# Output sums of a one-core hybrid mixer layer: residual put into the output first, sums added by accumulating transfers, three column blocks emptied by ACT

## What is computed

```
h = rms_norm(x, norm_g[l])
proj = jnp.einsum('bsd,dn->bsn', h, w_in[l])
...
y = jnp.concatenate([y_a, y_b, y_c], axis=-1)
x = x + jnp.einsum('bsm,md->bsd', y, w_out[l])
```

## Time and profile before

| | us |
|---|---|
| median of 3 runs (lowest, highest) | 1533.09 (1531.96, 1533.46) |
| the profiled execution's own time | 1533.12 |
| its span | 1531.3 |
| PE busy | 1524.5 |
| DVE busy | 1050.1 |
| ACT busy | 772.1 |
| POOL busy | 357.1 |

### The profile page before, as it was taken

One profiled execution on the slowest core, in us unless ns is written; L12 is line 12 of the kernel. 1 busy time (PEld: TensorE's weight loads), 2 busy tenths in 40 slices (PEclk: granted clock), 3 DMA queues, 4 the chain that ended last, 5 costly groups with the idle time before them and its releaser, 6 DMA issues.

```text
span 1531.3 us, 18915 instructions
## 1 busy us (share of the span) xinstructions
PE 1524.5 (100%) x6963; PEld 1260.9 (82%) x6963; DVE 1050.1 (69%) x1619; ACT 772.1 (50%) x1025; POOL 357.1 (23%) x605
## 2 busy tenths in 40 slices
PE   9999999999999999999999999999999999999999
PEld 7888888888888887888878888888888888878887
DVE  7647555566769855576579667676556888887884
ACT  6745444587544444554545545534345444454542
POOL 9041112230230040126420354345300011110000
PEclk9999999999999999999999999999999999999999
DMA  9886778886787675569755787798885666677665
GB/s 296 282 244 191 221 212 232 213 234 190 228 248 210 193 223 167 156 183 279 247 187 177 224 253 212 233 274 254 239 261 177 206 197 203 186 263 225 213 224 165
DMA packets 206268, 337.78 MB, mean 221 GB/s; under 512 B 53049, under 2 KB 60520, under 8 KB 205920
## 3 DMA queue, kind: packets, MB, share of 16 engines
q1 hardware_dynamic: 184784, 288.66, 62.2%
q0 software_dynamic: 21344, 47.90, 11.0%
q10 hardware_dynamic: 48, 0.02, 0.0%
HBM read 312.81 MB, written 23.49 MB: 220 GB/s over the span
## 4 chain that ended last, share of the span: by engine, by line
PE 94%; DVE 3%; ACT 1%; DMA 1%; issue 0%; ACTq 0%; DVEq 0%
PE acc L1167 28%; PE acc L1170 28%; PE acc L1169 28%; PE mix L1170 1%; PE mix L1167 1%; PE mix L1169 1%; DVE w_lo L1849 1%; PE mix L1274 1%; PE mix L1357 1%; DVE t_lo L1868 1%; DMA w_raw<-in_w_out_dram 1%; PE mix L1346 0%; PE mix L1267 0%; ACT w_hi L1498 0%; PE acc L1183 0%
## 5 line engine op out<-in xcount | busy, mean ns | idle before, releaser
L1849 DVE TENSOR_TENSOR w_lo<-w_raw,w_hi 128x1024 fp32r<-128x1024 f32 (+2 forms) x524 | 630.3, 1217 | 358.5 <-ACT w_hi L1498 354.7
L1498 ACT ACTIVATE w_hi<-w_raw 128x1024 fp32r<-128x1024 f32 (+2 forms) x524 | 544.0, 1049 | 454.2 <-PE acc L1170 363.6
L1167 PE MATMUL acc<-w_hi,op_hi 128*128 128x512 f32 (+1 forms) x1868 | 734.3, 393 | 0.3 <-DVE w_lo L1849 0.3
L1170 PE MATMUL acc<-w_hi,op_lo 128*128 128x512 f32 (+1 forms) x1868 | 726.9, 389 | 0.0
L1169 PE MATMUL acc<-w_lo,op_hi 128*128 128x512 f32 (+1 forms) x1868 | 726.7, 389 | 0.0
L1167 PEld LDWEIGHTS acc<-w_hi,op_hi 128*128 128x128 f32 x1868 | 350.8, 188 | 74.0 <-issue 1.3
L1170 PEld LDWEIGHTS acc<-w_hi,op_lo 128*128 128x128 f32 x1868 | 350.7, 188 | 73.5
L1169 PEld LDWEIGHTS acc<-w_lo,op_hi 128*128 128x128 f32 x1868 | 350.9, 188 | 71.0
L883 POOL DMA_DIRECT2D conv_dram<-y x48 | 30.7, 692 | 169.3 <-ACT y L1550 168.5
L883 POOL DMA_DIRECT2D y_dram<-y x32 | 20.5, 713 | 185.2 <-DVE y L2362 116.7
L1037 POOL DMA_DIRECT2D bp_dram<-b_ps x48 | 31.1, 694 | 68.6 <-ACT b_ps L1719 64.6
(11 more groups left out here) (467 smaller groups left out, 1295.2 us busy)
## 6 DMA issues: line engine op xcount, KB each, us to landing
w_raw<-in_w_in_dram SPq DMA_DIRECT2D x367, 512.0 KB, 4.6
w_raw<-in_w_out_dram SPq DMA_DIRECT2D x128, 512.0 KB, 4.4
w_raw<-in_w_in_dram SPq DMA_DIRECT2D x16, 384.0 KB, 3.2
w_raw<-in_a_wuq_dram SPq DMA_DIRECT2D x12, 512.0 KB, 5.1
conv_dram<-y POOLq DMA_DIRECT2D x48, 64.0 KB, 3.9
y<-conv_dram POOLq DMA_DIRECT2D x48, 64.0 KB, 4.7
w_raw<-in_a_wuqi_dram SPq DMA_DIRECT2D x6, 512.0 KB, 4.2
bp_dram<-b_ps POOLq DMA_DIRECT2D x48, 64.0 KB, 3.5
```

Source lines behind the costliest of these rows:

```text
L1167: nc.tensor.matmul(o, hi[:, kt, tok], hv[:, i, n0:n1], start=(kt == (kts if late else blk["kts"])[0]), stop=False)
L1170: last_mm = nc.tensor.matmul(o, lo[:, kt, tok], hv[:, i, n0:n1], start=False, stop=(kt == blk["kts"][-1]))
L1498: func(split_ap(w_hi, c), w_raw[:, c % RAW_BUFS, 0:n], ACT.Copy).then_inc(hi_ready, 1)
L1849: vec.tensor_tensor(split_ap(w_lo, c), w_raw[:, c % RAW_BUFS, 0:n], split_ap(w_hi, c).bitcast(F32), ALU.subtract).then_inc(lo_ready, 1)
```

## The change

POOL no longer loads x for seven of the eight column blocks. It copies those seven blocks of x straight into the output in DRAM, in two transfers (256 rows of 6144 bytes and 256 rows of 8192 bytes), where it used to load blocks 0 and 1, and afterwards adds every sum to the output in DRAM by accumulating transfers. Block 3 keeps its load, its adds on DVE and its stores by SP. The results of `out1` and `out2` for blocks 0 to 2 are copied from PSUM by ACT into two staging buffers (`out_stage`), each of which is free again once its accumulating transfer has landed; DVE had added them. `evs` no longer adds x: four DVE adds in place of eight. The two parts of blocks 0 to 2 are transferred one by one, so there are ten accumulating transfers of 512 KB where there were seven stores. The seven-product groups are the same, and so are PE's and SP's instructions.

```diff
-            for n in range(OUT_SINGLE):
-                if 512 * n == W_A:
-                    pool.wait_ge(y_lo_ready, KT // 2 - 4)
-                pool.dma_start(out_acc(n), x_dram[:, :, 512 * n:512 * n + 512]).then_inc(x_again[n], 16)
-            for n in range(2):
-                pool.wait_ge(a_y, 4 * n + 4)
-                y_blocks(n)
-            for p in range(2):
-                if p == 1:
-                    pool.wait_ge(y_lo_ready, KT // 2)
-                for q in range(2):
-                    n = OUT_SINGLE + 2 * p + q
-                    pool.dma_start(pair_sum(p)[:, :, 512 * q:512 * q + 512], x_dram[:, :, 512 * n:512 * n + 512]
-                                   ).then_inc(x_again[n], 16)
+            last_n = OUT_SINGLE - 1
+            for a, z in ((0, 512 * last_n), (512 * last_n + 512, D)):
+                pool.dma_start(out[0][:, a:z], x[0][:, a:z]).then_inc(out_done, 16)
+            pool.wait_ge(y_lo_ready, KT // 2 - 4)
+            pool.dma_start(out_acc(last_n), x_dram[:, :, 512 * last_n:512 * last_n + 512]).then_inc(x_again[last_n], 16)
+            pool.wait_ge(out_done, 32)
+
+            def add_out(k):
+
+                kind, n = ("out1", k) if k < last_n else ("out2", k - last_n)
+                wait_stored(pool, kind, n)
+                if k >= last_n:
+                    pool.wait_ge(out_added[(k - last_n) % 2], 16 * ((k - last_n) // 2 + 1))
+                pool.dma_start(out_dram[:, :, 512 * n:512 * n + 512], out_stage[k % 2], accum_op=ALU.add
+                               ).then_inc(out_added[k % 2], 16)
+
+            add_out(0)
+            add_out(1)
+            pool.wait_ge(a_y, 4)
+            y_blocks(0)
+            add_out(2)
+            pool.wait_ge(a_y, 8)
+            y_blocks(1)
...
-            for n in range(OUT_SINGLE - 1):
-                wait_stored(pool, "out2", n)
-                pool.dma_start(out_dram[:, :, 512 * n:512 * n + 512], out_acc(n)).then_inc(out_done, 16)
-            pool.wait_ge(out_done, 16 * (D // 512 - 1))
+            for k in range(last_n, 2 * last_n):
+                add_out(k)
+            for k in range(2):
+                pool.wait_ge(out_added[k], 16 * last_n)
+            pool.wait_ge(out_done, 16 * (2 + 4))
...
                 if kind in ("out1", "out2"):
+                    if arg == OUT_SINGLE - 1:
+                        return
+                    k = arg if kind == "out1" else OUT_SINGLE - 1 + arg
+                    if k >= 2:
+                        act.wait_ge(out_added[k % 2], 16 * (k // 2))
+                    act.wait_ge(acc_ready, b + 1)
+                    for m in range(M):
+                        ins = func(out_stage[k % 2][:, m, :], acc[b % 2][m][:], ACT.Copy)
...
                 wait_used(dve, last_seven(p))
-                for q in range(2):
-                    dve.wait_ge(x_again[n + q], again_count(n + q))
                 dve.wait_ge(first_kept, p + 1)
-                vec.tensor_tensor(c11, c11, u2, ALU.add)
-                step(vec.tensor_tensor(u2, p6, u2, ALU.add))
+                free(vec.tensor_tensor(u2, p6, u1, ALU.add), 2)
                 free(vec.tensor_tensor(u4, p5, u2, ALU.add), 0)
-                step(vec.tensor_tensor(u3, p7, u2, ALU.add))
-                step(vec.tensor_tensor(u2, p5, u3, ALU.add))
-                free(vec.tensor_tensor(c12, c12, u4, ALU.add), 1)
-                free(vec.tensor_tensor(c21, c21, u3, ALU.add), 2)
-                ins = vec.tensor_tensor(c22, c22, u2, ALU.add)
-                free(ins, 3)
+                free(vec.tensor_tensor(u3, p7, u2, ALU.add), 3)
+                free(vec.tensor_tensor(u5, p5, u3, ALU.add), 1)
```

More of the change, by code:

```diff
@@ L405, in hybrid_kernel @@
                                            ("t_lo", [P, 4, 512], F32R), ("sum45", [P, M, 1024], F32)])
+        out_stage = [acc0[:, :, 512 * k:512 * k + 512] for k in range(2)]
         par_in_ready = sem("par_in_ready")
@@ L512, in hybrid_kernel @@
         y_lo_ready = sem("y_lo_ready")
-        x_again = [sem(f"x_again{n}") for n in range(D // 512)]
+        x_again = [None if c in x_by_sp else sem(f"x_again{n}") for n, c in enumerate(X_MOVED)]
         s_summed = sem("s_summed")
@@ L520, in hybrid_kernel @@
         first_kept = sem("first_kept")
+        out_added = [sem(f"out_added{k}") for k in range(2)]
         last_parts = sem("last_parts")
@@ L586, in s_hi @@
         def s_hi(i):
[L587 removed]
+            return s_four[:, i - 8] if i < 12 else s_two[:, i - 12] if i < 14 else s_last[:]
         def s_lo(i):
@@ L606, in again_count @@
         def again_count(n):
-            return 16 * (9 if n < len(X_MOVED) and X_MOVED[n] not in x_by_sp else 1)
+            return 16 * 9
         def first_raw_dma(eng, i):
@@ L1503, in evac @@
                 if kind in ("out1", "out2"):
+                    if arg == OUT_SINGLE - 1:
[6 more added lines that the diff above has]
+                        ins = func(out_stage[k % 2][:, m, :], acc[b % 2][m][:], ACT.Copy)
+                        if m == 0:
+                            step(ins)
+                    ins.then_inc(acc_read[b % 2], 1)
                     return
@@ L1759, in evs @@
                 wait_used(act, last_seven(p))
-                func(part_sum[:, 0], seven_banks(p)[0], ACT.Copy).then_inc(first_kept, 1)
+                func(pair_sum(p)[:, 0, 0:512], seven_banks(p)[0], ACT.Copy).then_inc(first_kept, 1)
             pieces = dict(sh=sh, evs=evs, evac=evac, gt=gt, g2=g2, g4=g4, gb=gb, conv=conv, csq=csq, cn=cn, ce=ce, ca=ca, cv=cv,
@@ L1887, in evs @@
                 _, p5, p6, p7 = seven_banks(p)
-                u2, u4, u3 = part_sum[:, 0], part_sum[:, 1], part_sum[:, 2]
-                c11, c12, c21, c22 = [pair_sum(p)[:, m, 512 * q:512 * q + 512] for m in range(2) for q in range(2)]
-                n = OUT_SINGLE + 2 * p
-                b = pair_block(p)
+                u1, u4, u3, u5 = [pair_sum(p)[:, m, 512 * q:512 * q + 512] for m in range(2) for q in range(2)]
+                u2 = part_sum[:]
                 def free(ins, k):
@@ L1933, in evac @@
                 kind, arg = blk["kind"], blk["arg"]
+                if kind in ("out1", "out2") and arg < OUT_SINGLE - 1:
+                    return
                 if kind == "out1":
@@ L1951, in evac @@
                     vec.tensor_tensor(dst, late_bank()[:, 0:SEQ], dst, ALU.add).then_inc(last_out, 1)
-                elif kind == "out2":
-                    dve.wait_ge(acc_ready, b + 1)
-                    for m in range(M):
-                        ins = vec.tensor_tensor(out_acc(arg)[:, m, :], acc[b % 2][m][:], out_acc(arg)[:, m, :],
-                                                ALU.add)
-                        if m == 0:
-                            step(ins)
-                    ins.then_inc(acc_read[b % 2], 1)
                 elif kind == "az":
```

15 lines of the change are left out of this document (8 added, 7 removed).

## The result

| | before | after |
|---|---|---|
| median, us (lowest, highest; runs) | 1533.28 (1531.96, 1533.78; 4) | 1542.69 (1541.53, 1543.36; 4) |
| profiled execution, its span | 1533.12, 1531.3 | 1542.59, 1540.8 |

The ratio is 1.0064, 95% interval 1.0049 to 1.0079: slower by 9.4 us. The forecast was 1540.1 (1534.0 to 1549.0).

What follows compares the result with a forecast made beforehand. The prediction took PE to bound the kernel, busy 1524.5 of 1531.3 us. Copy +6.9, slow clock +1.0 and relief -0.9 sum to +7.0 on 1533.12, giving 1540.1 us, range 1534.0 to 1549.0.

Steps and rivals of the forecast that it cites:

- The copy, +6.9: Near 1115 us: 2560 KB more on q0 at 0.38 MB/us delay q1's weights, and PE waits 6.9 us longer.
- in packets it is the same: Behind `a_rows`: 512 packets before and now, if a row is one packet, so q1 gets as many turns.
- the wait of 6 to 9 us: Expected in the changed profile: PE waiting for `w_lo` near 1116 us, the largest wait of the run.
- ACT's 14 us: Expected in the changed profile at the copy: ACT waiting some 14 us at once for `w_raw`.
- the 17 us for the first weight transfer: Expected at the copy: the first weight transfer landing after some 17 us.
- PE after the stall, +1.0: Behind the copy's stall: PE's clock falls to half pace for 2.0 us, costing 1.0 us; bounds 0 and 3.8.
- The relief, -0.9: Seven-product stage: without the pairs' x loads, 0.9 of the 1.9 us PE lacks comes back; bounds 0 and 1.9.
- Accumulating, 0 (bound 8): Ten 512 KB accumulating transfers, 2.8 us each if cost doubles, were taken as free beside the weights; bound 8 us.
- the rival's 4 to 8 us: Accumulating makes weights late at the pairs or the last block late, adding 4 to 8 us: 1544 to 1548; chance 0.07.
- DVE and ACT, 0: Evacuations and `evs`: DVE loses 14 us of work, ACT gains 8.5, and neither costs or gains PE time.
- the copy would let the weights through: With 2 KB packets at the copy, weights share one for one and come 1.4 us late: 1533.6; chance 0.17.
- A slow copy (half rate): DRAM-to-DRAM copies run at half rate and block, costing 16.5 us: 1549.7; chance 0.07.

Runs made afterwards that it cites:

- half-early kernel: Changed kernel with only 1536 KB of the copy in place, the other 2048 KB as four later pieces, each after three more chunks: 1534.87 us, ratio 1.0011.
- paced kernel: Changed kernel with the copy as seven 512 KB pieces in 2 KB rows, one each three chunks, started later: 1533.85 us, ratio 1.0004; repeated 1533.31, 1.0.
- copy-only: Kernel before plus a spare 2560 KB copy of x behind the loads of blocks 0 and 1, nothing else of the change: 1541.38 us, ratio 1.0056.
- short-row: Changed kernel with the copy at the same place, issued as seven 512 KB transfers with 2 KB rows: 1543.01 us, ratio 1.0067.
- the one held behind `y_keep`: Changed kernel with its two large-row copies held until SP's last `y_keep` transfer has landed: 1538.1 us, ratio 1.0031.
- the one with the doubled sums: Seven-piece spread copy kernel, plus two more accumulating transfers of the first pair's sums into a spare DRAM table: 1539.34 us, ratio 1.0039.

## Why the prediction was right, and what was off

- **The copy, +6.9.** Right in mechanism, place and nearly in size: 5.8 us. The steps behind it held: a row of 8 KB is one packet, q1 takes as many turns as q0, it stands where it stood when q0 runs dry (3982 of `y_keep`'s 4096 runs had gone by then, 3999 before). q0 moved 1.47 MB in 4 us, 0.37 MB/us (0.38 was taken). One premise was wrong and did no harm: "in packets it is the same". The loads of x had gone in packets of two rows, not one (0.76 MB in 189 packets, 4.0 KB each), so the copy's 512 packets stood where 256 had stood, and a packet of the DMA view is not always one row. 1.1 us of the 6.9 did not come through. They fit the engines' time that q0 had left unused before: it held 74.6%, and 94.3% from 1104 to 1117 now. The half-early kernel bears this out: its 512 KB more, 1.4 us at 0.38, left ACT's wait at 7.3 us. Of the signs named ahead, the wait of 6 to 9 us was 5.8, ACT's 14 us were 13.2, q0 moved 4.68 MB from 1104 to 1117 (4.7 was named), and the 17 us for the first weight transfer were 13.8, since the transfer was issued later.
- **PE after the stall, +1.0.** The mechanism was right and the size wrong: 2.9 us. I took the length of the slow stretch from two rows at the program's start, 2.0 us. That was no length at all: the stretch at the start had begun with PE's first work and went on to 8.0 us (9.9 in the change's execution). It lasted about 6 us of work here. The upper bound, 3.8, held it. It is not a trait of this kernel alone: the copy-only and the short-row kernels show it after 5.9 us of standing (PEclk 0.66 and 0.68 from 1120 to 1130), the one held behind `y_keep` after 3.0, and the one with the doubled sums after 2.7. The Trainium skill ("TensorE: Matmul & The Clock Gate", section "Part 1: The HAM clock gate (the "warmup" mystery)") says that the clock falls when the array idles and rises again after sustained work; the trace agrees with the fall and shows 0.50 for 6 us of work.
- **The relief, -0.9.** Wrong: at most 0.1. The failed step is "without it 0.9 us comes back". I had read two idle gaps of DVE, 0.40 and 0.53 us, as the fault of POOL's loads. With those loads gone the paced kernel still has one of 0.82 us there, with the same w_hi behind it:

```profile
1357.87 1.22 DVE L1875 TENSOR_TENSOR w_lo<-w_raw,w_hi 128x1024 fp32r<-128x1024 f32 x1 [0.82 <-ACT w_hi L1513]
```

  ACT waits there for other work in its order (a PSUM tile of PE, 3.0 us from 1340 to 1380, one of DVE, 2.2), not only for weights (1.4, against 4.4 before). A gap before an instruction moves to the next cause when the first goes.
- **Accumulating, 0 (bound 8).** Right for the change: its trace has no such wait of PE. But there was hardly any slack under it. The step that a sum costs 2.8 us of the engines (two times 1.4) fell short: from 1416 to 1418 the summing alone held all engines at 0.18 MB/us, half of the 0.37 of the copy; 512 KB at that rate is 2.9 us, but with the start and the reads they landed in 5.6 to 10.5, and weights beside them were late by up to 3 us. The lower end of the rival's 4 to 8 us is what a doubled pair costs (4.3 of waits), a single one gives 0 to 1. The summing in the change, from 1416 to 1418:

```profile
q0 software_dynamic: 186, 0.36, 100.5%
q1 hardware_dynamic: 17, 0.03, 7.3%
```

  The last one is issued at 1528.93 and SP's last stores begin at 1537.44, so the end of the program is free of it, as worked out.
- **DVE and ACT, 0.** Right: 11.3 us less on DVE (14 reckoned) and 6.6 more on ACT (8.5 reckoned) changed no wait of PE, as the paced kernel shows (1532.1 of span against 1531.3).
- **The rivals.** That the copy would let the weights through needed 2 KB packets. None of the copies here went in such; the short-row kernel's were of 4 KB, for which I had reckoned 1537.7, and it took 1543.0, since the small runs at q1's head took the turns. So the way I counted `y_keep`'s runs was wrong, and 1533.6 for 2 KB packets remains untried. A slow copy (half rate) did not occur, and accumulating did not stall PE in the change.

The sum was 2.6 us short of the median: clock +1.9 and relief +0.8 under-counted, the stall 1.1 over, and the 0.7 of the start, 2.3 together. The stall's error hid part of the others', and the start's 0.7 is chance, read from one execution.

## What to carry to other kernels

A bulk transfer has no price of its own: it costs what the other queue's head loses while it runs, and what lead the consumer has left just there. So ask of each place how many turns the waiting queue needs until its urgent transfer is through (small runs ahead of it use up turns), how long a packet of the newcomer is against one of the urgent transfer, and how late the consumer already is. Split into short rows and spread over a stretch where the queue holds weights only, 3584 KB cost nothing measurable (1.0004 and 1.0); in two transfers at the tightest place they cost 9.4 us, a third of it from the clock that fell after the stall. Of the twelve experiments none beat the kernel before by more than its measurement can tell (0.9996 at best): sparing DVE and POOL time does not shorten a program that PE bounds. And a part that costs nothing in one place should be doubled before it is called free.

## What the hardware showed that was not expected

- Packets are not always rows: from DRAM to DRAM, rows of 2 KB went in pairs (4096 bytes), rows of 6 and 8 KB as they were, a wholly contiguous copy in pieces of 40 KB. Loads of x in 2 KB rows went in pairs on q0 too; the weights on q1, also in rows of 2 KB, did not. Turns between q0 and q1 were one for one at all these sizes (182 to 182, 19 to 19). The Trainium skill ("DMA: Bandwidth & Descriptors", section "SWDGE vs HWDGE vs iDMA") names 4096 B as a packet's preferred upper size; the 2 KB rows fit that, the other two do not.
- An accumulating transfer into DRAM moved 0.18 MB/us with all 16 engines held, against 0.37 for the copy. Its packets have 2048 bytes and took 203 ns on average (the first pair of the change, 1412 to 1424 us); the stores of the same sums before went in packets of 4096 bytes, 190 ns each. So q1 gets more turns beside it, and each byte costs twice as much; its issue on POOL took 1.16 to 1.24 us in the change, against 0.72 for a store.
- After 3.0 us of standing (and after 1.6 and 2.7 us, two microseconds apart) the granted clock fell as it did after 5.8, while three stands of 1.56, 0.64 and 0.93 us, some 4 us apart, left it at 1.00 in the profiled execution.
